# Hybrid decoder layer on one core: the first modulation and input products cut into two halves of the features, and the z units loaded earlier

## What is computed

```python
mod = (c @ w_ada[l] + b_ada[l]).reshape(B, N_MOD, D)      # c: 1 x 1024, w_ada: 1024 x 6144
sh1, sc1, gt1, sh2, sc2, gt2 = [mod[:, i, None, :] for i in range(N_MOD)]
h = rms_norm(x, g_norm1[l]) * (1.0 + sc1) + sh1
proj = h @ w_in[l]
dn_qkv, dn_z, dn_b, dn_a, fx_qkv, fx_f, gate_a, gate_b = jnp.split(proj, split_points, axis=-1)
qkv = jax.nn.silu(causal_depthwise_conv(dn_qkv, conv_w[l]))
```

## Time and profile before

| | |
|---|---|
| median of the runs | 1206.92 us |
| the profiled execution | 1205.64 us |
| its span, first to last instruction | 1203.8 us |
| mean granted TensorE clock | 0.984 |
| TensorE busy | 1110.9 us (92%) |
| DVE, ACT, POOL busy | 377.9, 208.3, 140.8 us |
| moved by DMA | 464.73 MB, mean 386 GB/s |

### The profile page before, as it was taken

One profiled execution on the slowest core, in us unless ns is written; L12 is line 12 of the kernel. 1 busy time (PEld: TensorE's weight loads), 2 busy tenths in 40 slices (PEclk: granted clock), 3 DMA queues, 4 the chain that ended last, 5 costly groups with the idle time before them and its releaser, 6 DMA issues.

```text
span 1203.8 us, 15193 instructions
## 1 busy us (share of the span) xinstructions
PE 1110.9 (92%) x6341; PEld 579.0 (48%) x6341; DVE 377.9 (31%) x702; ACT 208.3 (17%) x351; POOL 140.8 (12%) x61
## 2 busy tenths in 40 slices
PE   5999799999999999989898989899989999989896
PEld 2899699998343443433333334343434334333332
DVE  1687576474312132212121212122121222122202
ACT  2465536444000000000000000000000010000002
POOL 0775545820000000000000000000000000000000
PEclk9899899999999999999999999999999999999999
DMA  9982954869999999999999999999999999999996
GB/s 353 355 287 77 331 177 160 283 279 413 419 428 427 429 432 432 432 432 430 429 433 432 427 430 434 432 426 432 433 422 432 430 437 427 432 433 428 426 426 261
DMA packets 58901, 464.73 MB, mean 386 GB/s; under 512 B 7119, under 2 KB 34120, under 8 KB 37614
## 3 DMA queue, kind: packets, MB, share of 16 engines
q1 hardware_dynamic: 58028, 462.91, 93.0%
q10 hardware_dynamic: 786, 1.14, 0.3%
q0 software_dynamic: 48, 0.13, 0.0%
HBM read 463.13 MB, written 1.05 MB: 386 GB/s over the span
## 4 chain that ended last, share of the span: by engine, by line
PE 65%; DMA 28%; issue 2%; DVE 2%; ACT 2%; POOL 0%; ACTq 0%; SPq 0%; DVEq 0%
PE ps L530 63%; DMA ring<-in_w_down_dram 17%; DMA ring<-in_w_gate_up_dram 6%; DMA kept<-in_w_down_dram 4%; DMA ring<-in_w_in_dram 1%; PE ps L1031 1%; ACT kept L1423 1%; DMA ring<-in_g_onorm_dram 1%; PE ps L1063 0%; PE ps L538 0%; DVE ring L1592 0%; POOL w_lo L1983 0%; DVE ring L1531 0%; DVE ring L1601 0%; DVE ring L1590 0%
## 5 line engine op out<-in xcount | busy, mean ns | idle before, releaser
L530 PE MATMUL ps<-ring,kept 128*64 128x512 f32 (+2 forms) x2944 | 644.2, 597 | 33.1 <-DMA ring<-in_w_down_dram 20.3
L530 PEld LDWEIGHTS ps<-ring,kept 128*64 128x64 f32 (+2 forms) x2944 | 210.1, 138 | 441.6 <-issue 397.0
L530 PE MATMUL ps<-kept 128*128 128x128 f32 (+5 forms) x936 | 186.5, 415 | 8.3 <-ACT kept L1423 3.3
L530 PEld LDWEIGHTS ps<-kept 128*128 128x128 f32 (+2 forms) x936 | 102.4, 175 | 94.5 <-issue 81.0
L1419 ACT ACTIVATE kept<-kept 128x512 f32<-128x512 f32 x32 | 20.2, 630 | 723.1 <-DVE kept L1884 723.1
L1983 POOL TENSOR_TENSOR w_lo<-ring,w_hi 128x1024 fp32r<-128x1024 f32 x50 | 131.1, 2643 | 107.8 <-ACT w_hi L1200 107.7
L1884 DVE TENSOR_SCALAR kept<-ps 128x512 f32<-128x512 f32 x32 | 22.1, 692 | 378.7 <-PE ps L530 378.7
L1906 DVE TENSOR_TENSOR kept<-ps,kept 64x512 f32<-64x512 f32 x64 | 44.1, 689 | 296.0 <-PE ps L530 295.0
L530 PE MATMUL ps<-hT_hi,w_hi 128*128 128x256 f32 x304 | 89.4, 294 | 7.3 <-POOL w_lo L1983 7.3
L530 PE MATMUL ps<-hT_lo,w_hi 128*128 128x256 f32 x304 | 87.2, 287 | 0.0
L530 PE MATMUL ps<-hT_hi,w_lo 128*128 128x256 f32 x304 | 87.0, 286 | 0.0
(11 more groups left out here) (261 smaller groups left out, 711.7 us busy)
## 6 DMA issues: line engine op xcount, KB each, us to landing
ring<-in_w_gate_up_dram SPq DMA_DIRECT2D x52, 4096.0 KB, 28.0
ring<-in_w_down_dram SPq DMA_DIRECT2D x47, 2048.0 KB, 23.5
ring<-in_w_gate_up_dram SPq DMA_DIRECT2D x23, 2048.0 KB, 13.4
kept<-in_w_down_dram SPq DMA_DIRECT2D x16, 2048.0 KB, 24.6
ring<-in_w_ada_dram SPq DMA_DIRECT2D x24, 1024.0 KB, 8.8
ring<-in_w_in_dram SPq DMA_DIRECT2D x22, 1024.0 KB, 8.5
ring<-in_w_out_dram SPq DMA_DIRECT2D x4, 1024.0 KB, 6.5
ring<-in_w_o_fox_dram SPq DMA_DIRECT2D x2, 1024.0 KB, 7.3
```

The costliest lines, as they stand in the source:

```text
L530: return pe.matmul(dst, lhsT, rhs, start=start, stop=stop, skip_group_check=True)
```

## The change

`ada0` is loaded in two halves of the features: units 0 to 3 hold features 0 to 511 of shift and scale for two row blocks each, units 4 to 7 features 512 to 1023, each unit in two DMAs with 2 KB in a row. The dn units become 512 columns by half of the rows (dn 0 to 2 rows 0 to 511, dn 3 to 5 the rest), also with 2 KB in a row, and accumulate over both halves in six banks. The list now begins ada0 0 to 3, dn 0 to 2, ada0 4 to 7, dn 3 to 5. The first half of the modulation is summed on TensorE, the second half on DVE (8 instructions of 1024 columns) and over partitions on TensorE. h is formed and split in two halves. All dn units are split; none is multiplied in whole float32. The convolutions now wait for dn 3 to 5, half a unit each.

1/rms comes from x before its transposition (two squares with their sums on ACT, square root, reciprocal and a copy on DVE, two transposes). The masks lead SP's queue, and x is transposed ahead of the vectors.

The z units stand ahead of ada1 6 and 7 in the list, so z 0 takes the slot of fqk 2 and z 1 that of ada1 2. `add_rows(1, 4)` is moved ahead of the split of the cumulated rows; `ada_over_rows(1)` goes between the halves of z 1 and `mod_transposes(1)` between those of gates 0; `take_mod_rows(1)` and `take_mod(1)` on DVE go behind the attention matrix and behind `add_rows(2, 0)`. Its core:

```diff
-        UNITS = ada_part(0) + win_part("dn", 0, range(6))
+        UNITS = [("ada0", i, ada_first_unit(i)) for i in range(4)]
+        UNITS += [("dn", u, dn_unit(u)) for u in range(3)]
+        UNITS += [("ada0", i, ada_first_unit(i)) for i in range(4, 8)]
+        UNITS += [("dn", u, dn_unit(u)) for u in range(3, 6)]
         UNITS += ada_part(1, (0, 1)) + win_part("fqk", COL_FOX, (0, 1, 2)) + ada_part(1, (2, 3, 4))
         UNITS += win_part("fqk", COL_FOX, (3,)) + ada_part(1, (5,)) + win_part("fv", COL_FOX + 2 * W, (0, 1))
-        UNITS += ada_part(1, (6, 7)) + win_part("z", COL_Z, (0, 1))
+        UNITS += win_part("z", COL_Z, (0, 1)) + ada_part(1, (6, 7))
...
-                    if name not in SUMMED_NAMES:
+                    if name == "ada0" and 4 <= i < 7:
+                        sp.wait_ge(S("first_added"), 2 * (i - 4) + 3)
+                    elif name not in SUMMED_NAMES:
...
+            sp.dma_start(masks_kept, kept_masks).then_inc(S("x_in"), 16)
             sp.dma_start(xtok, x[0].rearrange("(t p) d -> p t d", p=P)).then_inc(S("x_in"), 16)
-            for n in range(KD):
+            for n in range(KD + 3):
                 stream(n)
             sp.dma_start(wsmall[:, :, 0:8], win3[:, :, COL_SMALL:COL_SMALL + 8]).then_inc(S("wsmall_in"), 16)
             sp.dma_start(wsmall[:, :, 8:12], win3[:, :, COL_F:COL_F + 4]).then_inc(S("wsmall_in"), 16)
-            for n in range(KD, KD + 6):
+            for n in range(KD + 3, KD + 6):
...
+            def ada_first(b):
+
+                for pair in range(4):
+                    w = unit_arrived(pe, "ada0", pair).rearrange("p (k q n) -> p k q n", k=2, q=4)
+                    for kk in range(2):
+                        k = 2 * pair + kk
+                        for q in range(4):
+                            last = mm(ps[32 * q:32 * q + 32, b, 0:256], cb[:, k, :], w[:, kk, q, :], k == 0, k == KD - 1)
                     last.then_inc(S("unit_used"), 1)
 
+            def ada_second(b):
+
+                pe.wait_ge(S("first_added"), KD)
+                w = unit_sb(UNIT_AT[("ada0", 7)]).rearrange("p (k q n) -> p k q n", k=2, q=4)
+                for q in range(4):
+                    last = mm(ps[32 * q:32 * q + 32, b, 256:512], km("ones")[:, 0:32], w[:, 1, q, :], True, True)
+                last.then_inc(S("unit_used"), 1)
+
+            def mod_transposes_first(half, b):
+                pe.wait_ge(S("mod_rows_sb"), half + 1)
+                for j in (2 * half, 2 * half + 1):
+                    last = pe.transpose(bank(b, j * P, P), mod_rows[:, j * P:(j + 1) * P], ident)
+                last.then_inc(S("mod_cols_ps"), 1)
...
                               rows == KD, True)
                 last.then_inc(S("ada_summed"), 1)
 
-            ada(0, 4, range(2))
-            pe.wait_ge(S("xsq_ready"), 1)
-            for k in range(KD):
-                last = mm(bank(5, 0, T), km("ones"), tmp.rearrange("p (k n) -> p k n", k=KD)[:, k, :],
-                          k == 0, k == KD - 1)
-            last.then_inc(S("xss_ps"), 1)
-            ada(0, 4, range(2, KD))
-            mod_transposes(0, 6)
+            ada_first(4)
...
+            def project_dn(u, ms):
+
+                half, c = divmod(u, 3)
+                lo = unit_r(UNIT_AT[("dn", u)]).rearrange("p (k n) -> p k n", k=4)
+                hi = hi_buf_r(u)
+                if u % 3 == 0 and ms[0] == 0:
+                    pe.wait_ge(S("hT_split"), half + 1)
+                for m in ms:
+                    if m % 2 == 0:
+                        pe.wait_ge(S("split_lo"), 2 * u + m // 2 + 1)
+                    cols = slice(m * P, (m + 1) * P)
+                    dst = bank(DN_BANKS[2 * c + m // 2], (m % 2) * T, T)
+                    for kk in range(4):
+                        k = 4 * half + kk
+                        for i, (w, x_part) in enumerate(((hi, hT_hi_r), (hi, hT_lo_r), (lo, hT_hi_r))):
+                            last = mm(dst, w[:, kk, cols], x_part[:, k, :], m % 2 == 0 and k == 0 and i == 0,
+                                      k == KD - 1 and i == 2)
+                    if m == 1:
+                        last.then_inc(S("half_used"), 1)
+                if ms[-1] == 3:
+                    last.then_inc(S("unit_used"), 1)
+
+            project_dn(0, range(4))
+            project_dn(1, range(4))
+            ada_second(4)
+            project_dn(2, range(2))
+            mod_transposes_first(1, 6)
+            project_dn(2, range(2, 4))
+            for u in range(3, 6):
+                project_dn(u, range(4))
+
+            pe.wait_ge(S("hT_split"), 3)
+            pe.wait_ge(S("conv_ready"), 3)
             for k in range(KD):
                 last = three_passes(ps[0:12, 2, 0:T], (wsmall_hi_r[:, k, :], wsmall_lo_r[:, k, :]),
                                     (hT_hi_r[:, k, :], hT_lo_r[:, k, :]), k)
...
-            pe.wait_ge(S("rowF_taken"), 1)
-            ada_over_rows(1, 5)
 
             pe.wait_ge(S("tok_taken"), 1)
             chunk_pairs((2, 7), kn, kn).then_inc(S("pairs_ps"), 1)
             pe.wait_ge(S("vb_ready"), 1)
             pe.wait_ge(S("unit_qk"), 1)
             chunk_pairs((3, 4), kn, qn).then_inc(S("pairs_ps"), 1)
-            project("z", 1)
-            mod_transposes(1, 6)
+            project("z", 1, (0,))
+            pe.wait_ge(S("rowF_taken"), 1)
+            ada_over_rows(1, 5)
+            project("z", 1, (1,))
 
             pe.wait_ge(S("X1_ready"), 1)
             for t in range(TT):
                 for h in range(H):
                     last = pe.transpose(bank((2, 7)[t], h * P, P), Xm[:, t, h, :], ident)
             last.then_inc(S("U1_ps"), 1)
...
+            def hT_half(half):
+                act.wait_ge(S("A1_ready"), half + 1)
+                for k in (4 * half + 2, 4 * half + 3):
+                    last = A(hT_first[:, k, :], hT_first[:, k, :], ACT.Identity, scale=A1[:, k:k + 1],
+                             bias=mod[:, k:k + 1])
+                last.then_inc(S("hT_high"), 1)
+                act.wait_ge(S("hT_low"), half + 1)
+                act.wait_ge(S("hT_high"), half + 1)
+                ks = slice(4 * half, 4 * half + 4)
+                A(hT_hi_r[:, ks, :], hT_first[:, ks, :], ACT.Copy).then_inc(S("hT_hi_ready"), 1)
+
+            hT_half(0)
+            for n in range(4):
+                split_hi(n, 0)
+                split_hi(n, 1)
+            hT_half(1)
 
             nproj = [0]
 
...
+            def hT_half(half):
+                dve.wait_ge(S("unit_used"), USED_AT[("ada0", 4 * half + 3)])
+                at = slice(256 * half, 256 * half + 256)
+                CP(mod_rows[:, at], bank(4, 256 * half, 256)).then_inc(S("mod_rows_sb"), 1)
...
+                for k in (k0, k0 + 1):
+                    last = TS(hT_first[:, k, :], hT_first[:, k, :], A1[:, k:k + 1], mod[:, k:k + 1], ALU.mult, ALU.add)
+                last.then_inc(S("hT_low"), 1)
...
+            hT_half(0)
+            for k in range(KD):
+                n = UNIT_AT[("ada0", 4 + k // 2)]
+                w = unit_sb(n)[:, 1024 * (k % 2):1024 * (k % 2) + 1024]
+                if k % 2 == 0:
+                    dve.wait_ge(S(f"slot_in{n % NSTREAM}"), ARRIVED[n])
+                if k == 0:
+                    last = TS(w, w, vec("c", k), None, ALU.mult)
                 else:
-                    dve.wait_ge(S("unit_used"), USED_AT[(f"ada{part}", KD - 1)])
-                CP(mod_rows, bank(b)).then_inc(S("mod_rows_sb"), 1)
-
-            take_mod_rows(0, 4)
-            take_mod(0, 6)
-            ins = STT(A1, mod[:, 8:16], 1.0, vec("g1", 0, KD), ALU.add, ALU.mult)
-            ins.then_inc(S("A1_ready"), 1)
-            dve.wait_ge(S("A1_ready"), 1)
-            for k in range(4):
-                last = TS(hT_first[:, k, :], hT_first[:, k, :], A1[:, k:k + 1], mod[:, k:k + 1], ALU.mult, ALU.add)
-            last.then_inc(S("hT_low"), 1)
-            dve.wait_ge(S("hT_hi_ready"), 1)
-            TTn(hT_lo_r, hT_first, hT_hi_r.bitcast(F32), ALU.subtract).then_inc(S("hT_split"), 1)
+                    dve.wait_ge(S("first_added"), k)
+                    last = STT(w, w, vec("c", k), prev, ALU.mult, ALU.add)
+                prev = w
+                last.then_inc(S("first_added"), 1)
+            hT_half(1)
...
-                dve.wait_ge(S("unit_used"), USED_AT[("dn", u)])
+                if u % 2 == 0:
+                    dve.wait_ge(S("half_used"), 3 + u // 2 + 1)
+                else:
+                    dve.wait_ge(S("unit_used"), USED_AT[("dn", 3 + u // 2)])
...
+            add_rows(1, 4)
...
-            for k in (4, 5):
-                add_rows(1, k)
+            add_rows(1, 5)
...
-            take_mod_rows(1, 5)
...
+            take_mod_rows(1, 5)
             TTn(qn, qn, exg, ALU.mult).then_inc(S("qd_ready"), 1)
+            add_rows(2, 0)
             take_mod(1, 6)
-            for k in range(2):
-                add_rows(2, k)
+            add_rows(2, 1)
```

(32 more changed lines are left out.)

165 lines of the change are left out of this document (78 added, 87 removed).

## The result

| | before | after |
|---|---|---|
| median of 4 runs each | 1207.28 us (1206.55 to 1208.91) | 1216.16 us (1214.65 to 1217.04) |
| the profiled execution, its span | 1205.64, 1203.8 us | 1214.65, 1212.8 us |
| mean granted TensorE clock | 0.984 | 0.973 |

The ratio is 1.007, with a 95% interval of 1.0053 to 1.0088: the change makes the kernel slower by 8.9 us. I had forecast 1195.4 us, in a range of 1190.5 to 1201, with a chance of 0.04 for slower. The forecast was wrong by more than 20 us, in sign too.

A forecast was written before the change was run, and what follows sets the result against it. The end was set by when the expert-weight stream starts, so by when the front, with PE as its chain, frees buffers. Gains of 10.0 (z units) and 1.5 us made 11.5, so 1195.4 us at the median, range 1190.5 to 1201.

The forecast's parts named there:

- The z part: Loading z 0 and z 1 ahead of ada1 6 and 7 ends PE's wait and low clock at z 0: 10.0 us gain.
- rival 3: z 0 finds a new wait, on ACT or POOL: half the term lost with the clock, 5 us, 1200.4; chance 0.07.
- The start: Start of the dn products: with 2 KB rows at 385 GB/s PE starts dn 0 at 26.1 us, against 32.37.
- The rule that a microsecond of dn 3 is a microsecond of DVE: At DVE's small products (L1553): every microsecond dn 3 starts later is one at the end; slower from a start of 59.5.
- the rule of the Trainium skill: At the row adds: two-SBUF-input DVE and SBUF-reading GpSimd instructions lock each other out; adds still taken at 1.2 to 1.5 us.
- rival 2: Every row add waits for POOL, 8 x 2.4 us; dn 3 starts at 56.0, total gain 3.5, 1203.4; chance 0.2, mostly milder.
- Rival 4: Slower at DVE's L1553: all eight adds and four wide ada1 adds wait for POOL, dn 3 at 61.6, 1209; chance 0.04.
- L1553 past 88: Sign against the forecast: DVE's small products taken later than 88 us, where 81 to 85 was expected.
- DVE holds it: Convolutions behind dn 3 put DVE 2.5 us later at L1553, so 1.5 of PE's 5.6 us gain are left.
- the first part: Front before the z units, with ada0 and dn loaded in halves: 1.5 us gain, with ends of -4 and +5.6.

The follow-up runs named there:

- z_only: The kernel before with only the z units ahead of ada1 6 and 7 in the load list, and their steps on PE and DVE moved along: 1198.91 us, ratio 0.9934.
- rows_on_pe: The kernel after with the second half of the modulation summed on PE, without the eight row adds on DVE: 1205.49 us, ratio 0.9992.
- short_pool2: The kernel after with POOL's six splits for dn 0 to 2 cut to 32 of 256 columns, most low parts left out: 1206.82 us, ratio 1.0004.
- pe_relief: rows_on_pe with the wsmall casts ahead of h's second half and two wide ada1 adds in DVE's wait for the exponentials: 1198.92 us, ratio 0.9949.
- dve_relief: The kernel after, eight adds kept, with wsmall casts moved earlier and two wide ada1 adds in DVE's wait for the exponentials: 1208.2 us, ratio 1.0027.
- late_split: pe_relief with the transposes directly behind the second half's sum, and dn 3 split on ACT only behind h's second half: 1198.59 us, ratio 0.9933.
- z_only_b: The same kernel as z_only, run again on the same chip as the best form of the first part: 1199.54 us, ratio 0.9937.

## Why the prediction was wrong

**What held.** The expert stage sets the end and keeps its rate. The z part: 10.0 us forecast, 9.0 at the mark, 7.6 in the median. I had let 2.7 us of it come from the clock at z 0; that came back, and 1.6 us went to a low clock in the router, a place that I had not looked at. There is no new wait at z 0 (rival 3), and in z_only no wait of PE for a moved step. The start: PE on dn 0 at 26.87 (26.1 forecast), 2 KB rows at 386 GB/s (385), the low clock for 5.3 us (6), a cast at 2.4 us beside POOL. The rule that a microsecond of dn 3 is a microsecond of DVE: from dn 3 to the small products the forecast had 35 us (83.0 - 48.0), the kernel after 35.8 (96.91 - 61.07), rows_on_pe 36.4 (88.71 - 52.35).

**The step that failed** is "The eight row adds are half as wide as those of L1531, 2.34 to 2.9 us each, so 1.2 to 1.5 and they keep up with the loads; the last two end at 40.5." They took 3.2 to 3.3 us each but for two, and the last ended at 50.8. dn 3 started at 61.07 instead of 48.0: 10.3 of these 13.1 us are the adds, and 2.8 arise behind them. 2.5 of those are the clock: at 1.2 GHz PE needed 1.0 us for ada_second and 4.8 for half of dn 2, against 0.5 and 2.9. I had quoted the rule of the Trainium skill that speaks against it (SBUF — State Buffer, Who interferes with whom) and had the cast of 2.36 us beside POOL in my rows, though that has one tensor operand where the rule as I quoted it speaks of two. Against it I set that POOL works in four instructions from 23.7 to 33.3 and then pauses. There is no such pause even for a POOL that no one delays: in rows_on_pe the fifth split follows the fourth at once, since half of a buffer is free when PE has used half of dn 0, and the sixth ends at 38.61. Beside the adds it is worse, because the waiting is mutual: POOL's instructions grew to 3.2 us, and its six splits filled the time to 41.84. The price I gave the rule in rival 2, 2.4 us for an add, was short as well. An add takes 3.25 beside POOL. Where the two take turns, a pair costs 3.25: one after the other without any overlap would be 1.30 + 2.39 = 3.69, so about a third of the add (0.44 of 1.30) lies beside POOL's instruction, and the rest does not. short_pool2 settles the cause: the same adds take 1.37 us when only POOL's instructions are made short.

**The other misses.** The adds are not the whole of it. In short_pool2 they end at 40.85, as forecast, and 8.8 us are missing at the mark all the same. 3.4 of them lie ahead of dn 3 (51.42 for 48.0): the step of four columns and the two scalings took 1.15 and 2.75 us beside POOL (0.16 and 0.74 in the kernel after, with POOL idle). 1.3 lie between dn 3 and the small products, 1.9 between these and the cumulated rows, 2.2 behind. In the 1.9 and its counterpart in the kernel after stands `add_rows(1, 4)`, which I had priced at 2.4. It took 4.38 beside POOL in short_pool2. In the kernel after, the wait fell into the instruction ahead of it: L1654 took 2.45 us where its counterpart took 0.16 before, and the add itself 2.35. The 2.30 of L1653 are not new. In the trace of before:

```profile
95.37 2.32 DVE L1572 SCALAR_TENSOR_TENSOR kept<-kept 128x8 f32<-128x8 f32 x1
```

**The sum, mended.** I had the mark at 193.82 - 11.5 = 182.3; it stands at 199.05, 16.7 later. 13.1 are the late dn 3, 0.8 arise between dn 3 and the small products, 2.1 between these and the cumulated rows (116.72 for 100.7), and 0.7 is left, near what the z part brought too little. Behind the mark 3.8 us come on top, 3.3 of them with a low clock.

**The rivals.** Rival 4 named the place (DVE at the small products) and the threshold (dn 3 at 59.5; it was 61.07), and 1209 for it; it needed "all of it at once" and had 0.04. It was the right mechanism, made to look unlikely by prices that were too low: with the adds ending at 50.8 and PE at 1.2 GHz behind them, dn 3 passed the threshold before the four wide adds had cost anything. The total came out higher than its 1209, about half of the difference being the 3.8 us behind the mark, which no rival had. Rival 2 has the right cause and too little of it. Of the forecast marks, L1553 past 88 was named as what would prove me wrong, and it came at 96.91.

**Is the lateness of DVE more than the adds?** Yes, and this only the runs showed. From z_only to after the mark moves by 14.2 us: taking the adds away gives 7.0 of them back (rows_on_pe), taking casts and two wide adds out of the chain 9.2 more (pe_relief, which lands 2.0 ahead of z_only's mark, little more than a mark moves between executions). I had seen the second in the forecast's "DVE holds it", at 5.6 - 1.5 = 4.1 us. Both had to go before the first part cost nothing, and with both gone it still wins nothing that can be measured.

Left open: the clock in the router and in the experts. The 82 matmuls take 16.3 to 16.4 us in ten of the thirteen profiled executions and 14.7 in before, dve_relief and late_split. The place of the mark does not decide it: late_split has its mark at 184.91 and 14.73 us, z_only and z_only_b have 184.84 and 184.97 and 16.35 and 16.36. In the experts, runs of 104 matmuls with 26.1 us change from one execution to the next of the same kernel: the chain of z_only has none, that of z_only_b has two. Why the clock falls was not tried.

## What to carry to other kernels

When DVE work with two SBUF operands is put beside a steady stream of GpSimd instructions, price both at nearly the sum of the two (here 3.25 of 3.69 us), lengthen GpSimd's as well, and only then ask where its pauses are. Before DVE is given work that frees another engine, lay out DVE's own time from there to the next place where someone waits for it; short instructions (casts, four-column steps) belong into GpSimd's idle time, wide ones into waits for other engines. A part of a change that moves load order is best tried alone: here it was the whole gain, and the other part, by itself, cost 14.4 us.

## What was not expected of the hardware

- Two alternating streams lengthen each other: DVE's add of 128 x 1024 from 1.30 to 3.25 us, GpSimd's subtraction of 128 x 1024 from 2.36 to 3.2.
- The size of the DVE instruction hardly matters to what it waits: beside GpSimd, 8 columns took 2.30 and 2.45 us, 96 columns 2.41, 4 columns 1.49, against 0.16 to 0.20 alone. One with a single tensor operand (a cast, a scaling by a column) is hit like one with two. The wait can also pass from one instruction to the next: 2.45 and 2.35 us for a step of 8 columns and the wide add behind it (after), 0.16 and 4.38 for the same two in short_pool2, where the step took its short time.
- A low clock in a busy stretch of unchanged code cost 1.6 to 1.7 us at a time. In the router two kernels with marks within 0.1 us of each other differ in it, and in the experts two executions of the same kernel do, so what is won in the front and what is seen at the end can differ by this much, and the runs do not say why.
